# The first expert ranking from unnormalised tokens, with the rest of tile 1 and the queries behind it

## What is computed

```python
ctx = ctx + mod_c[2] * yc                                   # yc: the mixer's output
hc2 = rms_norm(ctx, norm2) * (1 + scale) + shift            # "p0", one row of scale and shift for all tokens
q = (hc2 @ w_q).reshape(P_BLOCK, 8, 2, 64)                  # 8 heads, two half keys each
s = einsum('thpk,hpnk->thpn', q, sub_keys)                  # scores against 2 x 128 keys
s1, i1 = top_k(s[:, :, 0], 16); s2, i2 = top_k(s[:, :, 1], 16)
sc, pos = top_k(s1 + s2 over all pairs, 16)                 # 16 experts of 16384 for each token and head
gate = softmax(sc); act = gelu(einsum('td,thkd->thk', hc2, u_tab[idx]))
ctx = ctx + mod_c[5] * einsum('thk,thkd->td', gate * act, v_tab[idx])
```

## Time and profile before

| | us |
|---|---|
| median of 3 runs | 2463.06 (2463.0 to 2465.79) |
| the profiled execution | 2467.28 |
| its span, first to last instruction | 2465.5 |

### The profile page before, as it was taken

The page is one execution under the profiler, slowest core; times in us unless marked ns, Lnnn a source line. Parts: engine busy times, 40 slices in busy tenths (PEclk is TensorE's granted clock), DMA queues, the critical chain, the costliest instruction groups (busy, mean ns, idle before and its releaser), DMA issues.

```text
span 2465.5 us, 35630 instructions
## 1 busy us (share of the span) xinstructions
PE 1780.7 (72%) x13118; PEld 850.7 (35%) x13118; DVE 1631.1 (66%) x3826; ACT 972.8 (39%) x2655; POOL 966.9 (39%) x898
## 2 busy tenths in 40 slices
PE   7998988997886769456655666776977855555555
PEld 5877665553552225112221122221633411111111
DVE  1534457968998676577766676775486766666665
ACT  3311136744444333335433353453354433433333
POOL 4014123344444333444444444443043454444442
PEclk9999998999997889778887788887988987867776
DMA  9268769999999999999999999998489999999997
GB/s 354 75 252 333 283 285 388 420 421 420 380 401 423 421 422 391 415 421 421 421 421 421 418 421 420 417 396 349 168 368 421 420 422 420 422 421 421 419 417 297
DMA packets 127967, 938.60 MB, mean 381 GB/s; under 512 B 17168, under 2 KB 18192, under 8 KB 20784
## 3 DMA queue, kind: packets, MB, share of 16 engines
q0 software_dynamic: 114800, 807.34, 79.4%
q1 hardware_dynamic: 12992, 128.97, 13.2%
HBM read 935.10 MB, written 1.15 MB: 380 GB/s over the span
## 4 chain that ended last, share of the span: by engine, by line
DMA 41%; PE 36%; DVE 11%; issue 6%; ACT 5%; POOL 0%; DVEq 0%; SPq 0%; POOLq 0%; ACTq 0%
DMA arena<-in_experts,expert_cur 36%; PE ps L2199 13%; PE ps L1248 12%; DMA last_slot<-in_experts,expert_cur 4%; DVE arena L2281 4%; ACT diag L2092 2%; PE ps L1852 2%; PE ps L1260 2%; PE ps L1273 2%; PE ps L1484 1%; ACT coef L2087 1%; PE ps L1465 1%; ACT acts L2086 1%; PE ps L1890 1%; DVE last_slot L2281 0%
## 5 line engine op out<-in xcount | busy, mean ns | idle before, releaser
L2199 PE MATMUL ps<-arena,diag 64*64 64x512 f32 x5464 | 984.5, 768 | 545.8 <-ACT diag L2092 545.7
L2070 POOL DMA_INDIRECT arena<-in_experts,expert_cur x683 | 793.2, 1161 | 1144.0 <-PE ps L2199 913.6
L2281 DVE CUSTOM_DVE_ANT_0 arena<-arena 128x1024 f32<-128x1024 f32 x683 | 838.9, 1229 | 502.3 <-DMA arena<-in_experts,expert_cur 485.6
L2199 PEld LDWEIGHTS ps<-arena,diag 64*64 64x64 f32 x5464 | 237.6, 158 | 1116.8 <-ACT diag L2092 799.9
L2086 ACT ACTIVATE acts<-dots 128x2 f32<-128x2 f32 (+1 forms) x386 | 78.6, 204 | 990.4 <-DVE dots L2281 979.8
L2092 ACT ACTIVATE diag<-consts,coef 128x128 f32<-128x128 f32 x768 | 266.4, 393 | 12.5
L2199 PE MATMUL ps<-last_slot,diag 64*64 64x512 f32 x680 | 215.6, 763 | 49.6 <-ACT diag L2092 49.5
L2087 ACT ACTIVATE coef<-acts,gate_cur 128x1 f32<-128x1 f32 x768 | 185.1, 288 | 12.6
L1248 PE MATMUL ps<-wring 128*128 128x256 f32 (+2 forms) x568 | 146.1, 409 | 0.0
L2070 POOL DMA_INDIRECT last_slot<-in_experts,expert_cur x85 | 103.8, 1221 | 101.2 <-PE ps L2199 86.3
L2281 DVE CUSTOM_DVE_ANT_0 last_slot<-last_slot,arena 128x1024 f32<-128x1024 f32 x85 | 104.5, 1229 | 57.0 <-DMA last_slot<-in_experts,expert_cur 55.7
(11 more groups left out here) (406 smaller groups left out, 1996.0 us busy)
## 6 DMA issues: line engine op xcount, KB each, us to landing
wring<-in_w_mod SPq DMA_DIRECT2D x18, 2048.0 KB, 10.1
wring<-in_ev_w_in SPq DMA_DIRECT2D x14, 1024.0 KB, 9.2
arena<-in_w_mod SPq DMA_DIRECT2D x6, 2048.0 KB, 10.4
wring<-in_ev_w_in SPq DMA_DIRECT2D x6, 2048.0 KB, 13.8
arena<-in_experts,expert_cur POOLq DMA_INDIRECT x683
wring<-in_w_q SPq DMA_DIRECT2D x5, 2048.0 KB, 12.7
wring<-in_ev_w_out SPq DMA_DIRECT2D x3, 2048.0 KB, 12.8
arena<-in_ev_w_in SPq DMA_DIRECT2D x1, 2048.0 KB, 19.8
```

What stands on the lines that cost most here:

```text
L2070: nc.gpsimd.indirect_dma_start(ring_slot(slot), None, table, bass.IndirectOffsetOnAxis(ap=expert_cur[:, par, k:k + 1], axis=0),).then_inc( ...
L2199: last = nc.tensor.matmul(ps[rows_of(o), sum_bank(G // PH, odd, c), :], diag[rows_of(i), k % RING, rows_of(i)], ring_slot(RING_SLOT[G, k]) ...
L2281: ins = nc.vector.tensor_tensor_reduce(out=ring_slot(slot)[:, 0:D], in0=ring_slot(slot)[:, 0:D], in1=place, scale=1.0, scalar=0.0, op0=ALU ...
```

## The change

The ranking of head 0 of tile 0 no longer waits for the normed, turned tokens. With r the token's inverse root mean square, g the row (1 + scale) x gain and b the shift, the query is `((r x g) + b) W = r ((x g) W) + b W`. So x of tile 0 is turned as it is (`turn_x`), scaled by g while it is copied out of PSUM (g lies along the partitions there, as a column), and multiplied by `w_q` to "q0a"; b goes through `w_q` as one column for each head ("shift_q"), is spread over 128 columns and multiplied by the keys ("shift_s"). The raw score is brought out of PSUM by one VectorE instruction: score x r + shift_s.

- Columns: the modulation rows 6 to 9 (shift and scale of "p0") are also turned into columns in the first mixer, one turn on TensorE and one copy on VectorE for each (`later_mod_pe`, `later_mod_dve`).
- Order on TensorE: tile 0's output, turn of x, shift's query, q0a, shift's score, score; only then tile 1's turned yb and its output halves, the turns of both normed tiles, q0b and the query of head 2.
- VectorE: residual of tile 0, second half of the scaled copy, norm of tile 0, score, whole ranking of head 0, residual half of tile 1, 7 steps of the next ranking, other residual half, norm of tile 1. ScalarE takes all four copies of turned rows (before, VectorE took one).
- SyncE: w_q of layer 0 is loaded right behind the output weights, ahead of the gate row and of the rows of scale and shift.
- Gathers: the ring's order is changed so that the first five slots lie over nothing that is still read; the sixth gather waits for the norm of tile 1.
- `WOVEN` has 7 stages in place of 4 (queries of heads 3 to 7), `PACE` is 6 in place of 4.

```diff
-PACE = 4
+PACE = 6
@@ group_names / mixer_groups, s == 0
-        g += [("ybT", 0), ("out0", 0, 0), ("out0", 0, 1), ("ybT", 1), ("out0", 1, 0)]
-        g += [("ht", "p0", 0, h) for h in range(2)] + [("out0", 1, 1), ("q0a",)]
-        g += [("ht", "p0", 1, h) for h in range(2)] + [("s0", 0, 0), ("q0b",), ("q0", 0, 2)]
-        for h in range(3, WOVEN_FROM):
-            g += [("q0", 0, h), ("s0", h % 2, (h - 2) // 2)]
+        g += [("ybT", 0), ("out0", 0, 0), ("out0", 0, 1), ("xT", 0), ("shift_q",), ("xT", 1), ("q0a",)]
+        g += [("shift_s",), ("s0", 0, 0), ("ybT", 1), ("out0", 1, 0), ("out0", 1, 1)]
+        g += [("ht", "p0", t, h) for t in range(2) for h in range(2)] + [("q0b",), ("q0", 0, 2)]
-WOVEN_FROM = 6
-WOVEN = [[("q0", 0, 6)], [("q0", 0, 7), ("s0", 0, 2)], [("s0", 1, 2), ("s0", 0, 3)], [("s0", 1, 3)]]
+WOVEN = [[("q0", 0, 3)], [("q0", 0, 4), ("s0", 0, 1)], [("q0", 0, 5), ("s0", 1, 0)], [("q0", 0, 6), ("s0", 1, 1)],
+         [("q0", 0, 7), ("s0", 0, 2)], [("s0", 1, 2), ("s0", 0, 3)], [("s0", 1, 3)]]
@@ mixer_dma
             for c in range(2):
                 load_weight(sp, ("w_out0", s, c), T["ev_w_out"][c])
+            if s == 0:
+                for c in range(2):
+                    load_weight(sp, ("w_q0", s, c), T["w_q0"][c])
             wait_stored(sp, 5)
             sp.dma_start(m["gate"], mods[0, s, 2].partition_broadcast(P)).then_inc(bc_landed["g0", s], 16)
@@ mixer_act, s == 0
                 take_yb(0)
+                act.wait_ge(p0_column_taken, len(COLUMNS_P0))
+                bank = in_bank(act, ("xT", 0))
+                for k in range(4):
+                    last = A_(raw_xT[:, k, :], bank[:, k * P:(k + 1) * P], ACT.Copy, scale=mod_columns_p0[:, 1, k, 0:1])
+                free_bank(last, ("xT", 0))
+                shifts = in_bank(act, ("shift_q",))[:, 0:2]
+                free_bank(copy(shift_q, shifts.unsqueeze(2).broadcast_to((P, 2, P))), ("shift_q",))
                 norm(0)
+                free_bank(copy(raw_qT, two_heads(("q0a",))), ("q0a",))
+                free_bank(copy(shift_s, in_bank(act, ("shift_s",))), ("shift_s",))
                 take_yb(1)
+                gate_exp_act(act, 0)
                 norm(1)
@@ mixer_dve, s == 0
                 residual(0, 0)
                 residual(0, 1)
+                ...
+                    last = V.tensor_scalar(raw_xT[:, 4 + j, :], bank[:, j * P:(j + 1) * P],
+                                           mod_columns_p0[:, 1, 4 + j, 0:1], None, ALU.mult)
                 norm(0)
+                taken(dve, ("shift_s",))
+                free_bank(V.scalar_tensor_tensor(out=m["score"][:, 0, 0:2, :], in0=bank.rearrange("p (h n) -> p h n", h=2),
+                                                 scalar=rstd[:, e:e + 1],
+                                                 in1=shift_s.rearrange("p (h n) -> p h n", h=2), op0=ALU.mult, op1=ALU.add),
+                          ("s0", 0, 0))
+                rank_steps(RANKS[0], 0, RANK_STEPS)
                 residual(1, 0)
-                norm_take(dve, V.tensor_copy, "p0", 0, 1, 0, m["hT"])
+                rank_steps(RANKS[1], 0, RANK_EARLY)
                 residual(1, 1)
                 norm(1)
-                take_score(0, 0)
-                first_ranks_dve(RANKS[0:2])
@@ first_scores, TensorE
-                from_a(1, 0)
                 from_b(0, 0)
                 from_b(0, 1)
-                from_a(1, 1)
+                turn_x(0)
+                for h in range(2):
+                    last = accumulate(bank[:, h:h + 1], [(w_q[:, k, h * P:(h + 1) * P], mod_columns_p0[:, 0, k, 0:1])
+                                                         for k in range(KT)])
+                turn_x(1)
+                for half in range(2):
+                    taken(pe, ("xT", half))
+                    for h in range(2):
+                        for k in range(4 * half, 4 * half + 4):
+                            last = M(bank[:, h * P:(h + 1) * P], w_q[:, k, h * P:(h + 1) * P], raw_xT[:, k, :],
+                                     start=h == 0 and k == 0, stop=k == KT - 1, skip_group_check=True)
+                ...
                 turn_b(1)
+                for c in range(2):
+                    from_a(1, c)
+                    from_b(1, c)
+                for t in range(2):
+                    norm_pe(pe, "p0", t, m["hx2"][:, t, :])
+                ...
                 first_queries(1, ("q0b",))
-                for h in range(2, WOVEN_FROM):
-                    first_query_of_head(pe, h)
+                first_query_of_head(pe, 2)
@@ ring_order and sums_pool
-                        slot = (0, 1, 2, 3, 4, 5, 7, RING)[n % (NSLOT - 1)]
+                        slot = (1, 2, 3, 5, RING, 0, 4, 7)[n % (NSLOT - 1)]
+            if G == 0 and k == FREE_SLOTS:
+                pool.wait_ge(h_ready.sem, h_ready.count(("p0", 1)))
```

More of the change, by code:

```diff
@@ L313 @@
 N_COLUMNS = 4
+COLUMNS_P0 = range(6, 10)
 ROWS = 8
@@ L534, in build @@
         w_ab = small[:, 672:800].rearrange("p (k n) -> p k n", k=KT)
+        mod_columns_p0 = small[:, 912:944].rearrange("p (v k s) -> p v k s", v=2, k=KT)
+        raw_xT, raw_qT = area(0, KT, P, of=late), area(1024, 2, P, of=late)
+        shift_q, shift_s = area(1280, 2, P, of=late), area(0, 512, of=last_slot)
         mod_columns1 = small[:, 800:832].rearrange("p (s v k) -> p s v k", s=2, v=2)
@@ L1331, in first_queries, with turn_x @@
                     product.mark(last, name)
+                def turn_x(half):
+                    if half:
+                        pe.wait_ge(x_ready.sem, x_ready.count(("m0", 0)))
+                    else:
+                        pe.wait_ge(x_half_ready, 1)
+                    bank = out_bank(pe, ("xT", half))
+                    for j in range(4):
+                        c = (4 * half + j) * P
+                        last = TR(bank[:, j * P:(j + 1) * P], x[:, 0, c:c + P], const(IDENT))
+                    product.mark(last, ("xT", half))
+                wq = lambda: weights(pe, ("w_q0", s, 0)).rearrange("p (k n) -> p k n", k=KT)
                 from_a(0, 0)
@@ new lines, in first_scores @@
+                product.mark(last, ("q0a",))
+                taken(pe, ("shift_q",))
+                pe.wait_ge(bc_landed["keys0", s], 16)
+                for name, source in ((("shift_s",), shift_q), (("s0", 0, 0), raw_qT)):
+                    if source is raw_qT:
+                        taken(pe, ("q0a",))
+                    bank = out_bank(pe, name)
+                    for h in range(2):
+                        last = M(bank[:, 256 * h:256 * h + 256], source[:, h, :], m["keys"][:, h, :], start=True, stop=True)
+                    product.mark(last, name)
@@ L2034, in build @@
         SHORT_HEADS = 2
+        FREE_SLOTS = 5
         def ring_order():
```

78 lines of the change are left out of this document (49 added, 29 removed).

## The result

| | before | changed |
|---|---|---|
| median us (9 runs each, side by side) | 2463.06 | 2473.39 |
| lowest to highest | 2459.42 to 2467.07 | 2468.58 to 2482.03 |
| the profiled execution (its span) | 2467.28 (2465.5) | 2473.39 (2471.2) |
| TensorE / VectorE busy us | 1780.7 / 1631.1 | 1765.4 / 1631.4 |

The ratio is 1.0048, 95% interval 1.0036 to 1.0061: 11.8 us slower (8.9 to 15.0); the two medians differ by 10.3. The forecast was 2463.5 with a range up to 2470, so the time lies outside it.

The account below looks back on a forecast made before the run. DMA's gathers were taken as the bound, with VectorE bounding around 660 to 700 us. DMA -2.6, PACE +2.6 and columns +0.5 gave +0.5 us on 2463.06, so 2463.5 us; range for 8 in 10: 2453.5 to 2470.

Parts of the forecast that it names:

- Where the bound lies: Expert-row gathers fill DMA from 370 to about 1700 us, mostly 421 GB/s; only time DMA stands still can change.
- Change 1, the early ranking: Chain from tile 0's turn to the first gather: issued at 316.6 us, 14.4 us earlier.
- Loads: SyncE's queue with w_q0 ahead of the gate row: no cost, 5 us of cover.
- Change 2, five free slots: Gathers 0 to 4 go at once; gathers 5 to 7 wait for tile 1's norm and start at 330.8 us.
- Change 3, the weave: Woven stages in head 0: 6.2 us a pair, last score 376.6 us, gather 16 near 376.9.
- The sum in DMA: Transfers moved by 400 us: 28.3 against 27.3, so 2.6 us gained, with 10.4 us of idle stretches.
- the gap at the small projection: DMA's stall at 395 to 400 us, 3.8 us lost before, closes as TensorE has caught up.
- PACE: Three fewer blanks among the stages, 1.3 us lost each where VectorE bounds; two counted, 2.6 us lost (0 to 3.9).
- Columns: Four turns and copies in the first mixer, mostly hidden by the weight stream: 0.5 us lost (0 to 1.6).
- Gather 16 queued behind the last woven score: Rival: each us of the score past 376.6 costs one of DMA; 5 us late gives 2468.5 to 2469.8; chance 0.24.
- Gathers keep flowing: Rival: DMA's idle stretches of 10.4 us don't open; 2453.1 us, or 2458.3 for half; chance 0.28.
- The change doesn't do what it says: Rival: the first gather stays near 331 us because loads or columns come late; 2466 to 2469 us; chance 0.05.

Follow-up runs that it names:

- changed again: The changed kernel run again without an edit: +12.6 us (8.4 to 16.7) against the kernel before.
- w3: The changed kernel with PACE put back from 6 to 4: +12.8 us (7.9 to 17.5) against the kernel before.
- z6: The changed kernel with the shift's query made by 16 matmuls of 128 equal columns instead of one: +9.1 us (4.9 to 13.3) against before.
- x4: The changed kernel with 2 of the shift query's 16 one-column matmuls (wrong shift): +5.9 us (3.4 to 8.1) against before.
- x3: The changed kernel with gathers 0 to 4 also waiting for tile 1's norm: +10.6 us (6.9 to 14.0) against before.
- w4: The changed kernel with queries 3 to 5 and their scores back ahead of the first sum, and PACE 4: +11.6 us (7.4 to 15.8) against before.
- y3: The changed kernel with the keys' slot taken last and tile 1's norm ahead of the next ranking's early steps: +5.4 us (2.7 to 8.1) against before.
- y4: y3 with PACE 4 instead of 6: +2.0 us (-1.0 to 4.9) against the kernel before.
- y1: The changed kernel with the keys' slot taken last among the nine ring slots: +7.1 us (3.7 to 10.6) against before.

## Why the prediction was wrong, point by point

**Where the bound lies.** Right: in both profiles of the changed kernel the bytes account for the time from the anchor to the end to within a microsecond.

**Change 1, the early ranking.** I had the first gather 32.2 us behind the anchor (316.6 - 284.42). Measured: 31.9 where the clock stayed full, 33.5 (changed again) and 35.1 where it fell. The sum of full-clock rows was right; that the clock falls in it was missing. The 32 one-column records take 3.63 us at full clock, 113 ns each. The 25 ns that the Trainium skill (TensorE: Matmul & The Clock Gate, section "Wait — 56ns, not 53.3ns?") gives for small matmuls are a floor, and these records, each with weights of its own, lie more than four times above it; the forecast was right not to go by it.

**Loads.** Right in effect: SyncE's rows put the keys' issue at 279.88 in the changed kernel, 31 us before the first gather is issued at 311.72, and none of the chain's rows waits for a load.

**Change 2, five free slots.** The sixth gather was forecast 46.4 us behind the anchor; measured 49.3 and 47.6, and 46.0 in w3, whose clock stayed full. Right but for the clock.

**Change 3, the weave.** The pace of 6.2 us a pair held (gathers 8, 10, 12 and 14 stand 6.1 to 6.6 us apart). The end of the first pair's sum, which lets gather 8 go, was forecast 62.9 us behind the anchor (347.3 - 284.42); gather 8 came at 66.7 and 64.6, at 62.9 and 63.0 in w3 and z6 with their full clock. Gather 16 was forecast at 92.5 and came at 97.6 and 95.5, at 93.8 and 93.9 in w3 and z6; GpSimd did wait for the woven score. So the path through tile 1's norm, the queries and the first sum was forecast rightly for the full clock.

**The sum in DMA. Here it failed, in two terms.** Transfers moved from 20 us behind the anchor on, by windows of each trace; the forecast's row has its own counts, and behind 115.6 us 421 GB/s:

| up to, us behind the anchor | 94.8 | 115.6 | 150 |
|---|---|---|---|
| kernel before, measured | 20.5 | 27.4 | 40.8 |
| forecast | 20 | 28.3 | 42.1 |
| changed | 20.0 | 26.0 | 37.8 |
| changed again | 20.1 | 26.7 | 38.8 |
| w3 | 20.1 | 27.4 | 40.6 |
| z6 | 20.0 | 27.6 | 40.4 |

Up to 94.8 us the forecast is met to a tenth of a transfer, and nothing of the early start is left there even by its own count: the kernel before has moved 20.5. The gain of 1.0 transfer was to come behind it, from gather 16 on time and from the gap at the small projection, 3.8 us before, which "closes", since TensorE "has caught up and the ring is full of open gathers". It didn't. Windows of the changed kernel from 120 us behind the anchor:

```profile
396.62:411.62 15.00, 11.76 (x57) 8.35 (x54) 9.75 (x31) 9.73 (x20) 3.61 (x3) 0.66 0.88 367
411.62:426.62 15.00, 15.00 (x92) 9.39 (x91) 11.43 (x33) 7.69 (x18) 5.10 (x6) 1.00 0.91 328
```

They lose 2.1 transfers, 5.3 us, where the forecast counted none (1.8 in its second trace, 0.6 in w3, 1.0 in z6; the kernel before, whose gap lies ahead of these windows, loses 0.4 in them). Gathers come behind each other as fast as DMA takes them, but the sums stay just behind (VectorE is at 15.55 of 20 us from 380 on), so the 9 us without a sum between 396.85 and 405.89 (the rows of L2287 above) empty the queue. Second, the full clock in the chain: with gather 16 behind its forecast by 5.1 and 3.0 us, DMA moved 6.0 and 6.6 transfers from 94.8 to 115.6 us, not 8.3. Together the two put the changed kernel's traces 4.3 and 3.3 transfers, 11 and 8 us, below the forecast at 150 us.

What is not explained: w3 and z6, with a full clock in their traces, are level with the kernel before at 150 us (40.6 and 40.4 against 40.8) and miss only the gain, but their runs are at +12.8 and +9.1. So the clock is not shown to be what costs in the usual execution; a chain later by 1.6 and 3.2 us goes with 1.7 and 2.7 transfers less than in w3, but x4, with a full clock and the shortest chain, has 0.7 less than w3 in the ledger. And behind 150 us the changed kernel's traces lose 2.6 and 2.3 transfers more than the kernel before, some 6 us, of which PACE is the forecast's 2.6; the rest stays open.

So the early gathers themselves were not overrated: the forecast had shrunk 14.4 us to 2.6, and these 2.6 hung on the later gap alone. x3 shows that the early bytes bring nothing measurable, and w4 that the path through tile 1's norm and the queries, left whole ahead of the first sum, can cost all 11.6 us.

**PACE.** Forecast 2.6 us lost. Measured +3.9 alone and 3.4 between y3 and y4. In the ledger the nine traces with PACE 6 lose 4.5 transfers from 360 to 480 us on average, the nine with PACE 4 and at most seven stages 3.6: 0.9 transfers, 2.3 us. Right, as far as intervals of 3 to 4 us to either side can say. Only w3 shows nothing, with an interval that holds both.

**Columns.** Forecast 0.5, measured +1.0 (-1.7 to 3.4): nothing against it.

**Rivals.** "Gather 16 queued behind the last woven score" came true: gather 16 was 5.1 and 3.0 us late (the rival named 5), though part of the delay came from the clock in the chain to the first gather and not from the woven stages. It gave 2469.8 at most, since it was reckoned from the sum above, in which the gap at the small projection costs nothing. y1 prices the queue at about 5 us. "Gathers keep flowing" is refuted: DMA stood at 175 and 52 GB/s. "The change doesn't do what it says" is refuted by the first gather.

**What the loss is made of.** From +11.8 down, by the edits that took it away: the queue behind the score 5, the norm's place 2 to 3, PACE 3.4, together 10 or 11; the remaining 1 to 2 us are inside the measurement. The sum, from the changed kernel (+11.8) to y4 (+2.0), is far outside the noise; each part alone is known to some 4 us.

## What to carry to other kernels

When work is started earlier into a ring of buffers, the gain is not the time of the first transfer but that of the first one which needs a freed buffer; follow what frees it, and look there first for what to move (here the norm's place was worth 2 to 4 us). Before a wait is placed ahead of a gather on an in-order queue, see whether another buffer can take this turn: here another rotation of nine slots was worth about 5 us in the two kernels with the long weave, and nothing in the one without. A gap at which DMA stands still should only be counted as closed if the consumer is shown to be several buffers ahead, and a single profile should be anchored behind the part that wanders, and set beside its kernel's median: here five of nineteen traces caught the fastest execution.

## What the runs showed of the hardware

- **The granted clock can fall while TensorE stays busy.** In six of the eleven traces with all 16 one-column matmuls the mean clock of the 15 us that hold them (15 to 30 us behind the anchor) was 0.77 to 0.89 (TensorE busy 5.00 of 5 us in the windows at 0.71 and 0.61 above; by single microseconds it stands at the lower level, 0.50 or 1.2 GHz, from 293 to 298 us); in the other five, in both with 128 columns and in all six of the kernels without this part it was 1.00. The Trainium skill, TensorE: Matmul & The Clock Gate, section "HAM oscillation — how this bites in real kernels", puts falls down to waits between bursts; this case's trace shows one behind matmuls of one column that TensorE's row counts as busy: the last waits ahead of it are 0.21 and 0.68 us, at 280 to 282 us, and the traces that keep the full clock have the same rows. Two traces with the wide form are too few to call it shown that it keeps the clock.
- **The same first mixer takes 275 to 285 us up to the anchor**, with the columns in it (275.2 to 285.3) or without (276.6 to 285.3). Profiled times can differ by up to 10 us from this alone, as much as the effect that was to be explained.
- **A 128-column fp32 matmul against fresh weights costs nearly the same as a one-column one**: 3.74 (z6) against 3.63 us (w3) for 32 records. The broadcast over 128 columns cost TensorE 0.11 us here.
